# Splitting the last output-weight products into two k-halves, and laying two ring places out by the same halves

## What is computed

```
x = x + g_m * hybrid_mixer(h, w_in, ..., w_out)        # ends in m @ w_out
h = modulate(rms_norm(x, norm_ffn_g), sh_f, sc_f)
logits = h @ router_w + router_b                        # top-4 of 32 experts
# per expert e, on the tokens that chose it:
gu  = xs @ w_gate_up[e] + b_gate_up[e]                  # 1024 x 2048 weights
act = clamped_swiglu(gu)
y   = act @ w_down[e] + b_down[e]                       # 1024 x 1024 weights
out = rms_norm(x + g_f * weighted_sum(y), final_norm_g)
```

## Time and profile before

| what | value |
|---|---|
| median of three runs | 1168.23 us (1166.73, 1168.53, 1168.23) |
| the profiled execution | 1166.24 us |
| its span in the profile | 1164.5 us |
| mean granted TensorE clock | 0.953 of full speed |
| PE busy | 949.4 us, 82% of the span |
| DVE busy | 487.4 us, 42% |
| ACT busy | 400.2 us, 34% |
| DMA, mean over the span | 402 GB/s, 467.56 MB |

### The profile page before, as it was taken

The page is one execution under the profiler, slowest core; times in us unless marked ns, Lnnn a source line. Parts: engine busy times, 40 slices in busy tenths (PEclk is TensorE's granted clock), DMA queues, the critical chain, the costliest instruction groups (busy, mean ns, idle before and its releaser), DMA issues.

```text
span 1164.5 us, 23616 instructions
## 1 busy us (share of the span) xinstructions
PE 949.4 (82%) x9185; PEld 495.5 (43%) x9186; DVE 487.4 (42%) x1150; ACT 400.2 (34%) x773; POOL 8.9 (1%) x26
## 2 busy tenths in 40 slices
PE   6899999998989887887987875875875876876875
PEld 3799999853433333332332321321321322322323
DVE  0779797573443443342342421422422422322333
ACT  1544434424433342342442421421322322332233
POOL 0100000000000000000000000000000000000000
PEclk9999999999999999998998998998999998998998
DMA  9979786999999999999999999999999999999995
GB/s 361 389 277 353 289 321 242 426 422 425 406 423 426 426 427 427 426 427 427 426 426 427 426 426 427 426 426 427 426 426 426 427 426 426 427 426 429 425 426 216
DMA packets 60494, 467.56 MB, mean 402 GB/s; under 512 B 5196, under 2 KB 6516, under 8 KB 24628
## 3 DMA queue, kind: packets, MB, share of 16 engines
q1 hardware_dynamic: 60468, 467.19, 97.0%
HBM read 466.13 MB, written 1.05 MB: 401 GB/s over the span
## 4 chain that ended last, share of the span: by engine, by line
DMA 39%; PE 37%; SPq 10%; DVE 7%; issue 4%; ACT 2%; DVEq 0%; PEldq 0%; ACTq 0%
PE B L1310 22%; DMA trio<-in_w_down_dram 20%; DMA W<-in_w_down_dram 14%; PE B L1045 10%; SPq L393 6%; DMA raw<-in_w_in_dram 4%; SPq L395 3%; PE B L1319 2%; DVE wl L728 1%; PE B L1262 1%; DVE EW L984 1%; DVE EW L981 1%; DVE EW L978 1%; ACT EW L641 1%; DMA raw<-in_w_ada_dram 1%
## 5 line engine op out<-in xcount | busy, mean ns | idle before, releaser
L1310 PE MATMUL B<-W,trio 128*32 128x512 f32 (+1 forms) x4784 | 451.7, 522 | 102.2 <-DMA W<-in_w_gate_up_dram 83.8
L1310 PEld LDWEIGHTS B<-W,trio 128*32 128x32 f32 x4784 | 163.8, 113 | 367.7 <-issue 168.7
L651 ACT ACTIVATE mod<-EW 32x256 bf16<-32x256 bf16 x368 | 152.6, 415 | 235.0 <-DVE EW L998 227.2
L978 DVE TENSOR_SCALAR EW<-B 128x256 f32<-128x256 f32 x46 | 19.5, 424 | 376.6 <-PE B L1310 376.6
L641 ACT ACTIVATE EW<-EW 128x256 f32<-128x256 f32 x46 | 19.2, 416 | 324.7 <-DVE EW L978 324.7
L1045 PE MATMUL B<-hh,wh 128*128 128x256 f32 x384 | 109.6, 285 | 2.0 <-DVE wl L728 2.0
L1045 PE MATMUL B<-hl,wh 128*128 128x256 f32 x384 | 108.6, 283 | 0.0
L1045 PE MATMUL B<-hh,wl 128*128 128x256 f32 x384 | 108.6, 283 | 0.0
L1319 PE MATMUL B<-b_gu,trio 128*32 128x512 f32 x368 | 50.8, 621 | 66.6 <-issue 55.1
L535 ACT ACTIVATE wh<-raw 128x2048 fp32r<-128x2048 f32 x32 | 59.6, 1907 | 97.5 <-DMA raw<-in_w_in_dram 60.5
L996 DVE SCALAR_TENSOR_TENSOR EW<-B,stat,trio 128x256 f32<-128x256 f32 x46 | 22.3, 484 | 158.4 <-PE B L1310 158.4
(11 more groups left out here) (245 smaller groups left out, 825.6 us busy)
## 6 DMA issues: line engine op xcount, KB each, us to landing
W<-in_w_gate_up_dram SPq DMA_DIRECT2D x112, 2048.0 KB, 35.3
W<-in_w_down_dram SPq DMA_DIRECT2D x48, 2048.0 KB, 39.8
spare<-in_w_gate_up_dram SPq DMA_DIRECT2D x16, 2048.0 KB, 28.7
trio<-in_w_down_dram SPq DMA_DIRECT2D x15, 2048.0 KB, 41.5
raw<-in_w_in_dram SPq DMA_DIRECT2D x13, 2048.0 KB, 10.2
raw<-in_w_ada_dram SPq DMA_DIRECT2D x11, 2048.0 KB, 10.6
raw<-in_w_out_dram SPq DMA_DIRECT2D x2, 2048.0 KB, 8.2
W<-in_w_ada_dram SPq DMA_DIRECT2D x1, 2048.0 KB, 22.7
```

Of the source, the lines that this page charges most:

```text
L651: A(ys[CAP * m:CAP * m + CAP, g * QC:(g + 1) * QC], yp[CAP * g:CAP * g + CAP, m, :], ACT.Copy).then_inc(y_moved, 1)
L1310: t = M(o, src[:, k % KQ, CAP * (k // KQ):CAP * (k // KQ) + CAP], w, start=(first and k == 0), stop=(k == KT - 1))
```

## The change

The products of the last column half (h = 1) are taken in the ranges k 0 to 3 and k 4 to 7, no longer k 0 to 5 and k 6 to 7; those of h = 0 stay. A new semaphore `half_used` goes up by one when a tile a has finished its first range in h = 1. The ring places of the units 8 and 9 are no longer the pieces 5 and 6, `wh1` and `wl1`, but "first", which is the k 0 to 3 half of `wh1` with the k 0 to 3 half of `wl1`, and "second", which is the two other halves. So a partition's part of such a unit is two runs of 8 KB, 16 KB apart. Load 8 waits for `half_used` to be 2 and stands ahead of the wait for `mix_done` to be 4; loads 9 and 10 stay behind that wait. The view of the gate/up source is kept in two dimensions for this.

```diff
-        PLACE = ("spare", 0, 1, 8, 9, 2, 3, 4, 5, 6, 7, "trio")
+        PLACE = ("spare", 0, 1, 8, 9, 2, 3, 4, "first", "second", 7, "trio")
...
+            if where in ("first", "second"):
+                return slot(5, 2).rearrange("p (s g n) -> p s g n", s=2, g=2)[:, :, ("first", "second").index(where), :]
...
-        gu_v = w_gate_up[0].rearrange("e (g p q) n -> e g p (q n)", p=P, q=KQ)
+        gu_v = w_gate_up[0].rearrange("e (g p q) n -> e g p q n", p=P, q=KQ)
...
-                    sp.dma_start(unit_pair(u).rearrange("p g n -> p (g n)"), gu_v[e, j]).then_inc(s_unit[u % SLOTS], 16)
+                    sp.dma_start(unit_pair(u), gu_v[e, j]).then_inc(s_unit[u % SLOTS], 16)
...
             load(7, 1)
+            sp.wait_ge(half_used, TA)
+            load(8, 1)
             sp.wait_ge(mix_done, TA * NH)
-            load(8, 1)
             load(9, 1)
...
-                for ks in (range(0, KT - 2), range(KT - 2, KT)):
+                for ks in (range(0, KT - 2), range(KT - 2, KT)) if h < NH - 1 else (range(0, KT // 2), range(KT // 2, KT)):
...
                         if ks[-1] == KT - 1:
                             t.then_inc(mix_done, 1)
+                        elif h == NH - 1:
+                            t.then_inc(half_used, 1)
```

More of the change, by code:

```diff
@@ L266, in hybrid_trunk @@
         wts_ready = sem("wts_ready"); rank_done = sem("rank_done"); wT_done = sem("wT_done")
-        wT_ready = sem("wT_ready"); table_ready = sem("table_ready"); order_ready = sem("order_ready"); list_ready = sem("list_ready"); c_order = sem("c_order"); x_added = sem("x_added"); y_zero = sem("y_zero"); pos_moved = sem("pos_moved"); over_ready = sem("over_ready")
+        wT_ready = sem("wT_ready"); table_ready = sem("table_ready"); order_ready = sem("order_ready"); list_ready = sem("list_ready"); c_order = sem("c_order"); x_added = sem("x_added"); half_used = sem("half_used"); y_zero = sem("y_zero"); pos_moved = sem("pos_moved"); over_ready = sem("over_ready")
         yw_ready = sem("yw_ready"); st_ready = sem("st_ready"); y_cut = sem("y_cut"); y_rest = sem("y_rest"); y_moved = sem("y_moved"); y_low = sem("y_low"); gf_used = sem("gf_used")
```

## The result

| | before | changed |
|---|---|---|
| median of 20 runs each | 1167.83 us | 1170.13 us |
| profiled execution | 1166.24 us | 1170.15 us |
| its span | 1164.5 us | 1168.4 us |

The ratio is 1.0017, with a 95% interval of 1.0011 to 1.0023: 2.0 us slower (1.3 to 2.7), where +1.8 was forecast; the two medians are 2.3 us apart.

A forecast was written before the change was run, and what follows sets the result against it. From about 204 us the stream of expert weights (DMA) was taken as the bound. Halved runs +2.1, order of products -0.3 and early load 0 made +1.8 us on 1168.23: 1170.0 us, 8-in-10 range 1167.2 to 1172.2.

The forecast's parts named there:

- The halved runs: Units 8 and 9 in the weight stream: 28 units after 318 us at 0.076 us each, +2.1 us (1.9 to 2.4).
- periods: Time of the weight stream for twelve units, forecast to rise from 59.03 to 59.19 us.
- The price taken from the down units: Weight stream: 128 more runs cost 0.076 us a unit, from down units' 4.970 us against gate/up units' 4.894.
- The order of the products: Mixer's last column half: DVE finishes earlier, routing and the stream's restart come sooner, -0.3 us (0 to -0.7).
- The steps inside the mixer: End of the mixer: DVE's operations for the last two tiles start at 233.63 and 236.37 us.
- The early load: Load 8 issued near 230 us instead of 236.35: only lengthens a full queue, moves no byte sooner, 0 us.
- The sum: Whole kernel: 2.1 - 0.3 = +1.8 us, on a median of 1168.23 giving 1170.0 us, +0.15%.
- the release after the stop: Third expert: PE frees the first unit, ending SP's wait on the full ring, near 317.9 us instead of 318.17.
- the runs are free: Rival on the halved units: source still one 16 KB run, nothing added, only -0.3 remains, 1167.9 us; chance 0.18.
- a split destination costs by itself: Rival on the halved units: destination split adds to source split's cost, 0.152 us a unit, 1172.2 us; chance 0.12.
- the stream gains: Rival: early load and earlier routing close the hole at 318 us, runs free, at most 1.5 us, 1166.7; chance 0.05.

The follow-up runs named there:

- layout-only kernel: The changed kernel with the old order of the products and load 8 back behind the fourth mix_done: 1169.54 us, ratio 1.0014 to the kernel before.
- order only: The kernel before with only the last column half taken in k 0 to 3 and k 4 to 7: 1168.14 us, ratio 1.0000.
- down in one run: The kernel before with the down weights' source read as one 16 KB run per partition, output not the reference's: 1164.57 us, ratio 0.9972.
- loads late: The kernel before with loads 8, 9 and 10 moved behind the wait for x_added: 1174.35 us, ratio 1.0059.
- both kernels again: The changed kernel and the kernel before, each unchanged and profiled once more; the span of the kernel before was 1169.0 us.

## Why the prediction was right

**The halved runs: +2.1 forecast, +2.2 measured.** B is 846.33, 846.59 and 846.60 in the three profiles with the old layout, 848.40, 848.87, 848.52 and 849.01 in the four with two halved units: 848.70 less 846.51 is 2.2 us. Their periods are 59.18 to 59.21, for a forecast of 59.19. The price taken from the down units held for units split on the other side; that it would was a choice between two values in the forecast, and the count of packets now says why.

**The order of the products: -0.3 forecast, -0.15 measured.** The steps inside the mixer came within 0.02 us. The size was off behind them: PE had its transposes done only 0.18 us sooner, and ACT waited for them. I had read 0.3 to 0.4 there, as if eight transposes from 238.63 on took 0.8. That 0.8 was the time from their start to the start of the next row; their own time stands in the same row as 1.03, and in the changed kernel they took 1.07 (from 238.95). Since the term is small, the sum did not suffer.

**The early load: 0 forecast, 0 measured,** with the stream at the same rate whether the load is issued at 230 or at 237 us.

**The sum.** 2.2 - 0.15 = +2.0 us, and the ratio says +2.0. That the forecast of 1170.0 us met the median of 1170.13 so closely is in part luck: it stood on a median of three runs, 1168.23, where twenty give 1167.83, and the 0.4 too much there made up for most of what the +1.8 fell short of the 2.3 between the medians. The profile's 3.9 us are 0.32 (a later start) + 1.66 (the fall of the clock: A 121.72 against 120.06) - 0.15 + 2.07 (B). One step of the forecast I read wrongly in its certainty: I had the release after the stop near 317.9 us, as if A were a constant of the kernel. It is not; see below.

**The rivals.** That the runs are free fell with the layout-only kernel and the period. The Trainium skill's page "DMA: Bandwidth & Descriptors", section "Why small descriptors are slow (HBM only)", would have had 0.3 us in all by its 32 bytes a descriptor, which was my estimate from it; it left out the fixed overhead of about 3 cycles a packet that the same section names. The runs show 2.2, and the measurement decides. That a split destination costs by itself, on top, fell with the period, which rose by 0.076 us a halved unit and not by 0.152, and with the unit to `trio`, split in the destination alone, which kept the price that it had when it was split in both. That the stream gains fell with the kernel without the early load.

What stays open is what decides whether the clock falls ahead of the stop. In the profiles it fell once there (changed, order only, down in one run, loads late), twice (both kernels again), or not (the other seven), and in the two kernels that I profiled twice it differed between the two profiles of one program.

## What to carry to other kernels

When a stream of transfers is the bound, count its runs: a layout that frees a buffer sooner is paid for on every transfer that uses it, here on 28 units, for a start that a full queue made worthless. Before moving a load forward, look whether the queue is dry where it would go, and for the next place where the ring is full, because what is won ahead of it may be lost there. And cut a profile at such a place: the part behind it repeated to 0.6 us while whole spans of one kernel differed by 4.5.

## What the runs showed of the hardware

- A large load costs by its number of contiguous runs even at 16 KB: 16 KB, 8 KB and 4 KB runs came at 428.5 (4.894 us a unit), 422 and 409 GB/s, about 0.6 ns for each further run. It is equal whether the source, the destination or both are split, as is the number of packets on the profile's page. Over all kernels B follows that number: 18432 more packets, 16128 of them behind the stop, are 9.45 us of B (843.28 to 852.73), 0.59 ns each.
- TensorE's granted clock fell to half for 3.4 or 6.8 us at places that move from one execution to the next. Behind the stop, where PE waits for weights and its mean granted clock from 330 to 1130 us was 0.93 to 0.95, B repeated to 0.6 us, so it costs nothing that B shows; ahead of the stop a single fall cost 1.6 to 1.7 us and the two together 4.0 to 4.1. This is likely the larger part of the spread of the 20 runs of the kernel before (1165.82 to 1171.82), though I have no profile of each of them.
- Float32 matmuls whose moving operand is read in pairs of 8 bytes, 16 bytes apart, took 0.36 us more for 64 of them (7.44 against 7.08 us).
